# A block of state-space scan, gated mixer and experts: the head of the front stage and the segment sums of the scan are computed in another form and on other engines

## The reference

```python
mod_l = (silu(c) @ ada_w + ada_b);  mod_c = (silu(c_ctx) @ ada_w + ada_b)
xm = rmsnorm(h, norm1_w) * (1 + sc1) + sh1              # for both token sets
xbc, dt_raw = xm @ w_in[:, :2048], xm @ w_in[:, 2048:2080]
xs, bm, cm = split(silu(dwconv_centred(xbc, conv_w, conv_b)))   # 3 taps over the tokens
dt = softplus(dt_raw + dt_bias)                         # 2 directions x 16 heads
# per direction, in chunks of 128 tokens, the context's chunks first:
a_cum = cumsum(dt * A)                                  # A negative
decay[i, j] = exp(a_cum[i] - a_cum[j])  for j <= i, else 0
y_diag = sum_j (cm[i] . bm[j]) * decay[i, j] * dt[j] * x[j]
y_off  = (cm[i] . h_in) * exp(a_cum[i])
h      = h * exp(a_cum[end]) + sum_j bm[j] * exp(a_cum[end] - a_cum[j]) * dt[j] * x[j]
```

## Time and profile before

| | us |
|---|---|
| median of three runs | 3674.97 |
| the profiled execution | 3683.1 |
| its span | 3681.3 |
| TensorE busy | 3352.1 |
| VectorE busy | 1264.4 |
| ScalarE busy | 950.4 |
| GpSimd busy | 276.1 |

### The profile page before, as it was taken

How to read it: one execution, slowest core, us unless ns; L and a number is a source line. 1 busy time by engine, 2 the same in 40 slices (tenths; PEclk the granted TensorE clock), 3 DMA queues, 4 the chain that set the end, 5 groups by cost and what they waited for, 6 DMA issues and landing times.

```text
span 3681.3 us, 36826 instructions
## 1 busy us (share of the span) xinstructions
PE 3352.1 (91%) x14704; PEld 2224.6 (60%) x14704; DVE 1264.4 (34%) x1876; ACT 950.4 (26%) x1555; POOL 276.1 (7%) x241
## 2 busy tenths in 40 slices
PE   5888896999599999799999989999899899989997
PEld 3547643444443443377567858878677477768875
DVE  2237411101301011445433453323454533453334
ACT  2121102000200000244453323221344533232212
POOL 0006302000100000111111000000021111000000
PEclk7997898999799999899999989999899999999998
DMA  5001043220399999321111222223311012322221
GB/s 203 23 9 60 30 169 121 92 88 26 130 385 409 409 409 409 121 69 48 47 52 61 89 70 96 92 82 102 71 58 59 25 62 69 97 69 92 93 86 62
DMA packets 266761, 436.79 MB, mean 119 GB/s; under 512 B 10336, under 2 KB 180704, under 8 KB 265824
## 3 DMA queue, kind: packets, MB, share of 16 engines
q1 hardware_dynamic: 266448, 432.54, 33.3%
q0 software_dynamic: 144, 1.90, 0.1%
HBM read 432.32 MB, written 2.10 MB: 118 GB/s over the span
## 4 chain that ended last, share of the span: by engine, by line
PE 51%; DVE 4%; ACT 2%; DVEq 1%; issue 1%; ACTq 0%; DMA 0%; POOLq 0%; SPq 0%; POOL 0%
PE bank L1879 42%; PE bank L1940 2%; PE bank L1957 1%; PE bank L1976 1%; PE bank L1916 1%; PE bank L1526 1%; DVE ring_r L2211 1%; PE bank L1971 1%; ACT ring_r L2080 1%; PE bank L1946 1%; DVE x L1557 0%; DVE layers_norm_rstd L1554 0%; DVE layers_work L2330 0%; DMA ring<-in_w_in 0%; DVE x_r L1568 0%
## 5 line engine op out<-in xcount | busy, mean ns | idle before, releaser
L1879 PE MATMUL bank<-experts_x_hi_r,ring_r 128*128 128x512 f32 x1720 | 575.5, 400 | 7.0 <-DVE ring_r L2211 7.0
L1879 PE MATMUL bank<-x_r,ring_r 128*128 128x512 f32 x1376 | 545.7, 397 | 0.0
L2211 DVE TENSOR_TENSOR ring_r<-ring,ring_r 128x2048 fp32r<-128x2048 f32 (+2 forms) x162 | 324.4, 2002 | 427.8 <-ACT ring_r L2080 426.6
L1879 PE MATMUL bank<-layers_work_r,ring_r 128*128 128x512 f32 x1312 | 392.3, 401 | 9.2 <-DVE layers_work_r L2354 9.2
L2080 ACT ACTIVATE ring_r<-ring 128x2048 fp32r<-128x2048 f32 (+2 forms) x162 | 272.7, 1684 | 495.3 <-PE bank L1879 475.4
L1879 PEld LDWEIGHTS bank<-experts_x_hi_r,ring_r 128*128 128x128 f32 x1720 | 323.6, 188 | 109.5 <-issue 25.2
L1879 PE MATMUL bank<-ring_r 128*128 128x512 f32 (+1 forms) x1224 | 388.0, 378 | 0.0
L231 PE MATMUL bank<-xm,ring 128*128 128x512 f32 (+1 forms) x832 | 321.3, 546 | 0.0
L1879 PEld LDWEIGHTS bank<-layers_work_r,ring_r 128*128 128x128 f32 x1312 | 249.5, 190 | 78.5 <-DVE layers_work_r L2354 10.1
L1879 PEld LDWEIGHTS bank<-x_r,ring_r 128*128 128x128 f32 x1376 | 258.6, 188 | 62.6 <-issue 1.0
L2403 POOL TENSOR_TENSOR layers_p<-layers_p,layers_recip 128x512 f32<-128x512 f32 (+2 forms) x160 | 145.3, 925 | 1446.8 <-DVEq L2257 1446.8
(11 more groups left out here) (319 smaller groups left out, 4048.3 us busy)
## 6 DMA issues: line engine op xcount, KB each, us to landing
ring<-in_w_in SPq DMA_DIRECT2D x54, 1024.0 KB, 5.3
ring<-in_w_ffn_in SPq DMA_DIRECT2D x44, 1024.0 KB, 5.1
ring<-in_w_gate SPq DMA_DIRECT2D x30, 1024.0 KB, 18.4
ring<-in_w_in SPq DMA_DIRECT2D x14, 2048.0 KB, 8.1
ring<-in_w_down SPq DMA_DIRECT2D x28, 1024.0 KB, 18.5
ring<-in_w_up SPq DMA_DIRECT2D x26, 1024.0 KB, 18.2
ring<-in_ada_w SPq DMA_DIRECT2D x12, 2048.0 KB, 8.7
mixer_kept<-in_w_down SPq DMA_DIRECT2D x24, 1024.0 KB, 18.5
```

Source lines behind the costliest of these rows:

```text
L1879: last = pe.matmul(out, lhs, rhs, start=start and k == 0, stop=stop and k == len(pairs) - 1)
L2211: dve.tensor_tensor(r32(tile), tile, r32(hi), ALU.subtract).then_inc(done, 1)
```

## The change

In `front`: the fourth modulation slab goes to `core.x` and the first slab of w_in to `a.y`, which are idle there, so neither waits for a ring slot; the dt weights come as an array of long rows (1 KB a partition) that is laid out ahead. The sum of squares and the dt product run in four column strips, k-tile by k-tile, with the tokens as the streaming operand; the strips are folded by one product with ones (squares) or turned and added (dt, `turn_dt` and VectorE's `step`). Context squares go to VectorE. x is multiplied by the reciprocal root ahead of the modulation's factors, and what follows them is one tensor_scalar (latent) or one ACTIVATE (context) a k-tile. ScalarE copies the modulation's rows. The softplus runs beside column 1.

In `scan`: the eight curves of 16 heads (4 chunks, 2 directions) are made once by TensorE from a dta spread over 32 partitions a group (`strewn`). Per step ScalarE spreads one curve over four columns of a block diagonal (`stairs`), and `sums_of` is four products of 32 rows and 512 columns with ones. The segments move from VectorE to ScalarE, as Relu(acum - sum) and Exp(-...), and the mask moves into cm . bm, which VectorE multiplies by a triangle once per chunk and direction (`masked`). `sums_of(u+1)` moves between the two halves of `diag(u)`. `xdt` and `xend` get buffers of their own. The two masks leave the constants.

```diff
...
+    ada_w3 = core.x
+    xbc_w0 = a.y[:, :, :].rearrange("p t f -> p (t f)").rearrange("p (k n) -> p k n", k=KD)
...
+    core.slabs.begin(ada[:3] + xbc[1:])
...
+            for s in range(3):
                 load_slab(core, sp, ("ada", s), w_tiles(I["ada_w"], 0, D, 512 * s, 512))
-            load_slab(core, sp, "dtw", w_tiles(I["w_in"], 0, D, XBC, 2 * HEADS))
-            for s in range(4):
+            sp.dma_start(dt_w[:, :, :], I["w_dt"].rearrange("p (k n) -> p k n", k=KD)).then_inc(ada_in, 16)
+            sp.dma_start(ada_w3[:, :, :], w_tiles(I["ada_w"], 0, D, 512 * 3, 512)).then_inc(ada_in, 16)
+            sp.dma_start(xbc_w0, w_tiles(I["w_in"], 0, D, 0, 512)).then_inc(xbc_in, 16)
...
+                rows = slice(32 * (k % 4), 32 * (k % 4) + 32)
+                for name, sq_done, lo, hi in (("sq_l", sq_x, 0, T), ("sq_c", sq_ctx, T, TA)):
+                    pe.wait_ge(sq_done, k + 1)
+                    last = pe.matmul(core.ps(name)[rows, 0:hi - lo], core.c("mean_d")[:, 0:32], squares[:, k, lo:hi],
+                                     start=k < 4, stop=k >= 4)
...
+            pe.wait_ge(strips_kept, 2)
+            for name, lo, hi in (("rms_l", 0, T), ("rms_c", T, TA)):
+                core.banks.vacant(pe, name)
+                pe.matmul(core.ps(name)[:, 0:hi - lo], core.c("ones"), strips[:, 0, lo:hi], start=True, stop=True)\
...
+                else:
+                    pe.wait_ge(ada_in, 32)
...
-            for t in range(TT + CT):
-                last = product(pe, core.ps("dt")[:, t * 32:t * 32 + 32],
-                               [a.xm[:, k, t * P:(t + 1) * P] for k in range(KD)],
-                               [w[:, k, :] for k in range(KD)],
-                               core.slabs.done(("ada", 3)) if t == 0 else None)
...
+            for k in range(KD):
+                rows = slice(32 * (k % 4), 32 * (k % 4) + 32)
+                for name, xm_done, lo, hi in (("dt_l", xm_x, 0, T), ("dt_c", xm_ctx, T, TA)):
+                    pe.wait_ge(xm_done, k + 1)
+                    last = pe.matmul(core.ps(name)[rows, 0:hi - lo], dt_w[:, k, :], a.xm[:, k, lo:hi], start=k < 4, stop=k >= 4)
...
+            for s in range(4):
+                core.banks.filled(act, ("ada", s))
+                if s >= 2:
+                    core.banks.filled(act, ("adt", s - 2))
+                act.activation(ada_rows[:, s % 2, :], core.ps(("ada", s))[:, :], ACT.Identity).then_inc(core.banks.done(("ada", s)), 1)
+                act.drain().then_inc(ada_kept, 1)
...
+                act.activation(a.xm[:, k, T:TA], a.xm[:, k, T:TA], ACT.Identity, scale=scale1[:, k, 1:2],
+                               bias=core.mod[:, k, 1:2]).then_inc(xm_ctx, 1)
...
+            dve.reciprocal(rstd[:, :], rstd[:, :])
+            dve.drain()
+            dve.wait_ge(x_in, 16)
+            for k in range(KD):
+                dve.tensor_tensor(a.xm[:, k, :], a.xm[:, k, :], rstd[:, :], ALU.mult)
...
             for k in range(KD):
-                for j, (lo, hi) in enumerate(((0, T), (T, TA))):
-                    dve.scalar_tensor_tensor(out=a.xm[:, k, lo:hi], in0=a.xm[:, k, lo:hi],
-                                             scalar=scale1[:, k, j:j + 1], in1=rstd[:, lo:hi],
-                                             op0=ALU.mult, op1=ALU.mult).then_inc(scaled, 1)
...
+                dve.tensor_scalar(a.xm[:, k, 0:T], a.xm[:, k, 0:T], scale1[:, k, 0:1], core.mod[:, k, 0:1], ALU.mult, ALU.add)\
...
+                for name, t0, n in (("dt_tl", 0, TT), ("dt_tc", TT, CT)):
+                    core.banks.filled(dve, name)
+                    dve.tensor_reduce(raw[:, t0:t0 + n, :], core.ps(name)[:, 0:n * P].rearrange("p (t j h) -> p t h j", t=n, j=4),
+                                      AX.X, ALU.add).then_inc(core.banks.done(name), 1)
...
+                dve.tensor_tensor(raw, raw, dt_bias.unsqueeze(1).broadcast_to([P, CT + TT, 2 * HEADS]), ALU.add)
...
-    cb = spare[:, 0:TT * GROUPS * P].rearrange("p (t n) -> p t n", t=TT)
-    xdt, xend = spare[:, 2 * D:3 * D], spare[:, 3 * D:4 * D]
+    cb = spare.rearrange("p (d t g j) -> p d t g j", d=2, t=TT, g=GROUPS)
+    xdt, xend = core.sb("xdt", [P, D], ctx), core.sb("xend", [P, D], ctx)
...
+    curve = strewn[:, :, :, :, :].rearrange("p t d g r -> p (t d) (g r)")
+    stair = core.sb("stair", [P, HPG, P], ctx)
...
     core.slabs.begin(MIXER_SLABS)
...
+            for n in (0, 1):
+                core.banks.vacant(pe, ("curve", n))
+                for q in range(4):
+                    td = 4 * n + q
+                    last = pe.matmul(core.ps(("curve", n))[:, q * P:(q + 1) * P], curve[:, td, :],
+                                     core.c("tri_b" if td % 2 else "tri_f"), start=True, stop=True)
+                last.then_inc(core.banks.put(("curve", n)), 1)
...
             def sums_of(u):
-                d, t, _ = steps[u]
+                pe.wait_ge(stair_done, order[u] + 1)
                 for g in G:
                     core.banks.vacant(pe, ("seg", u, g))
-                    for r in range(HPG):
-                        col = d * HEADS + g * HPG + r
-                        last = pe.matmul(core.ps(("seg", u, g))[:, r * P:(r + 1) * P],
-                                         a.dta[:, t, col:col + 1].broadcast_to([P, P]),
-                                         core.c("tri_b" if d else "tri_f"), start=True, stop=True)
-                    last.then_inc(core.banks.put(("seg", u, g)), 1)
+                    rows = slice(32 * g, 32 * g + 32)
+                    pe.matmul(core.ps(("seg", u, g))[:, :], core.c("ones")[rows, :], stair[rows, :, :], start=True, stop=True)\
+                      .then_inc(core.banks.put(("seg", u, g)), 1)
...
-                if u + 1 in outs:
-                    sums_of(u + 1)
...
+                    if half == 0 and u + 1 in outs:
+                        sums_of(u + 1)
...
-            for n in range(len(outs) * GROUPS):
-                act.wait_ge(seg_done, n + 1)
-                act.activation(seg[:, n % NSEG, :], seg[:, n % NSEG, :], ACT.Exp).then_inc(decay_done, 1)
+            for n in (0, 1):
+                core.banks.filled(act, ("curve", n))
+                act.activation(curve[:, 4 * n:4 * n + 4, :], core.ps(("curve", n))[:, :].rearrange("p (q j) -> p q j", q=4), ACT.Identity)\
+                   .then_inc(core.banks.done(("curve", n)), 1)
...
+            def stairs(u):
+                d, t, _ = steps[u]
+                for r in range(HPG):
+                    act.activation(stair[:, r, :], curve[:, 2 * t + d, :], ACT.Identity, scale=core.c("stair")[:, r:r + 1])
+                act.drain().then_inc(stair_done, 1)
...
+                    for r in range(HPG):
+                        col = d * HEADS + g * HPG + r
+                        last = act.activation(seg[:, n % NSEG, r * P:(r + 1) * P], core.ps(("seg", u, g))[:, r * P:(r + 1) * P],
+                                              ACT.Relu, bias=acum[:, t, col:col + 1], scale=-1.0)
+                    last.then_inc(core.banks.done(("seg", u, g)), 1)
+                    act.drain()
+                    act.activation(seg[:, n % NSEG, :], seg[:, n % NSEG, :], ACT.Exp, scale=-1.0).then_inc(decay_done, 1)
+                if u + 1 in outs:
+                    stairs(u + 1)
...
-            def segments(u):
...
-                        last = dve.scalar_tensor_tensor(
-                            out=seg[:, n % NSEG, r * P:(r + 1) * P], in0=core.ps(("seg", u, g))[:, r * P:(r + 1) * P],
-                            scalar=acum[:, t, col:col + 1], in1=core.c("mask_b" if d else "mask_f"),
-                            op0=ALU.subtract, op1=ALU.add)
...
+            def masked(t):
+                core.banks.filled(dve, ("cb", t))
+                for d, tri in enumerate(("tri_f", "tri_b")):
+                    last = dve.tensor_tensor(cb[:, d, t, :, :], core.ps(("cb", t))[:, :].rearrange("p (g j) -> p g j", g=GROUPS),
+                                             core.c(tri).unsqueeze(1).broadcast_to([P, GROUPS, P]), ALU.mult)
+                last.then_inc(core.banks.done(("cb", t)), 1)
...
-            segments(first)
+            for t in range(first, TT):
+                masked(t)
+            dve.drain().then_inc(cb_done, 1)
...
-                if u + 1 in outs:
-                    segments(u + 1)
...
-                    cbg = cb[:, t, g * P:(g + 1) * P].unsqueeze(1).broadcast_to([P, HPG, P])
+                    cbg = cb[:, d, t, g, :].unsqueeze(1).broadcast_to([P, HPG, P])
...
+            pool.memset(strewn[:, :, :, :, :], 0.0).then_inc(strewn_zero, 1)
...
-        "tri_f": lower.T, "tri_b": lower, "mask_f": np.where(lower.T > 0, 0.0, NEG), "mask_b": np.where(lower > 0, 0.0, NEG),
+        "tri_f": lower.T, "tri_b": lower,
+        "stair": (np.arange(P)[:, None] % 32 == np.arange(HPG)[None, :]).astype(np.float32),
...
+    g["w_dt"] = f("w_in")[0][:, XBC:XBC + 2 * HEADS].reshape(KD, P, 2 * HEADS).transpose(1, 0, 2).reshape(P, -1)
```

(50 more changed lines are left out.)

198 lines of the change are left out of this document (93 added, 105 removed).

## The result

The changed kernel takes 3630.9 us (median of 4 runs, 3628.9 to 3633.5) beside 3676.4 for the kernel before (4 runs, 3674.3 to 3679.7): 45.5 us faster, ratio 0.9876, interval 0.9859 to 0.9893. The forecast was 3615, range 3596 to 3643: sign and range held, the gain was a quarter less than the 60 us forecast. Its profiled execution took 3630.0, span 3628.2.

A forecast was written before the change was run, and what follows sets the result against it. The prediction took the front's head to wait on a chain and the scan on hand-overs between engines. Front -33 and scan -27 gave -60 from the median 3675.0, so 3615 us, range 3596 to 3643.

The forecast's parts named there:

- Front: All work ahead of the scan: earlier slab, shorter scaling and turned dt product save 33 us, bounds -36 and -17.
- rival B: Front's dt product: column strips don't overlap, as each feeds two banks; front -17, total -44, 3631 us; chance 0.08.
- The root's slack: Front: reciprocal root and its products end at 38, hidden before the factors at 43.3 with 5 us to spare.
- the slab's 3.5 us: Front: the last modulation slab, no longer waiting for a ring slot, lets TensorE begin at 37.2 instead of 40.75.
- Scan: Scan stage: 126.6 us in place of 153.6, so -27; -44 at a period of 9.6, +4 at 16.4.
- The head: Scan's start: the first step's fourth decay product ends 38.2 us into the stage.
- Period: Scan step: a ring of ScalarE's segments, stair and TensorE's sums, 11.3, plus 0.7 for half clock: 12.0 us, bounds 9.6 and 16.4.
- the tail: Scan's end: half a diagonal 1.0, addition 0.7, L801 2.35 and hand-overs, together 4.4 us.
- a sign of being wrong: Scan: the prediction is wrong if the output steps' additions are 15 us or more apart.
- Rival A: Scan keeps its pace through half-clock spells or a ring through scaled x; scan -3, total -36, 3639 us; chance 0.15.
- Rival C: Scan: GpSimd's bound, a period of 9.6 us, is reached; scan -44, total -77, 3598 us; chance 0.12.
- Rival D: Scan: Relu and Exp in different tables, two loads of 1.28 a group; scan +55, total +22, 3697 us; chance 0.03.

The follow-up runs named there:

- experiment 11: The changed kernel with the fourth modulation slab loaded through the ring again: 3631.2 us, ratio 0.9875 to the kernel before.
- Experiment 4: The changed kernel with two buffers in turn for `part`, the second in a free context tile of x: 3617.4 us, ratio 0.9835 to the kernel before.
- experiment 8: The changed kernel with two `part` buffers, GpSimd's skip products in its waits and each step's fourth decay product on VectorE: 3629.7 us, ratio 0.9869 to the kernel before.
- experiment 5: The changed kernel with two extra TensorE products ahead of the wait for each of the 32 decay products: 3639.5 us, ratio 0.9897 to the kernel before.

## Why the prediction was right in sign and its gain 15 us too large

**Front: -33 forecast, -33.1 in the first trace, -31.5 on average.** Slab at 38.0 (37.2), factors at 42.3 (43.3), tiles ready at 46.4 (47.2), first column product at 47.7 (49.5). The average sets the eleven profiled executions with the new front (scan's first pass at 241.2) against the three with the old one (272.7). The 1.8 us are the clock: in this execution the last slab's 16 passes ran at full (1.92), where the forecast kept half (3.62), and the dt product's last passes did too (1.25 behind the last tile; the forecast's 2.3 lies between its 1.3 and 2.6 without a reason given). In the eleven the slab's passes took 1.92 in four and 2.9 to 3.6 in seven, and the first column product starts at 47.7 to 51.1, mean 49.5. The strips do overlap, over two banks too (32 passes in 4.59, for which one after another would be 10.4): rival B is refuted. The root's slack was 5 us as forecast (VectorE ends its products at 37.3). What the forecast left out is the half clock behind the wait ahead of the third column product, +1.7; from the first column product to the scan the new front takes 1.0 more than the old one, where the forecast's terms say 0.7 less. So the -33.1 of this trace is in part luck: 1.8 too good, 1.7 too bad. And the cause named for the slab's 3.5 us, a place of its own, was not needed (experiment 11). On average the slab came 2.5 earlier (38.5 against 41.1): near the size, not by the mechanism.

**Scan: -27 forecast, -20.2 measured.** The head was right (first step's fourth decay product ends 37.6 into the stage, forecast 38.2). ScalarE's costs came out below the forecast: four segments in 1.13 (1.3), 1.74 a group (2.1), stair 1.26 (1.4). TensorE's sums took 1.13 at full clock, as forecast (1.1), and 2.09 at half. The step that failed is **Period**: "A ring of waits: ScalarE's segments (8.4), its stair (1.4), TensorE's sums to the first bank read", 11.3, and 12.0 us with its 0.7 for half clock. The mean was 12.6 (fourth decay products end at 276.8 and 364.9, seven periods), though ScalarE needs only 4 x 1.74 + 1.3 = 8.3, not 8.4 + 1.4 = 9.8, and was idle for 46 of 101 us: with its pieces as measured that ring would have been 8.3 + 1.5 = 9.8. That 12.0 came so near 12.6 is luck: a ring priced too high stood in for one left out. What set the pace was a ring that the forecast didn't price: GpSimd's addition, VectorE's `part`, and behind it the bank of the fourth sum and scaled x. Experiment 4 removes it and the stage falls to 116.3, below the 126.6 forecast. So 4.1 of the 6.7 us that the stage is too long are the period; 3.3 are the tail, 7.7 in place of 4.4, its diagonal at half clock (6.56), and the head gives 0.6 back. The steps are uneven too: the additions stand 5.4 to 15.9 apart, one over the 15 that the prediction named as a sign of being wrong.

Rival A named lost pace by half-clock spells or by a ring through scaled x; it went over a quarter of that way (7 of 24 us), through another buffer. Rival C, GpSimd's list as the bound, is what experiment 4 points to once the buffer is doubled, at 11.1 and not 9.6, for the decay products cost 1.73 each beside a busy VectorE and 1.24 where it mostly waits (4.95 for four at 333.94 in the changed kernel); experiment 8, which shortened that list, got slower by another path and so didn't confirm it. Rival D: no table load stands among Relu and Exp.

The Trainium skill (TensorE: Matmul & The Clock Gate, on the measured speedup of small-K matmuls) gives 3.07x for four 32-row tiles. The trace agrees: eight passes one after another would be 8 x 0.43 = 3.5 us, and they took 1.13 at full clock, 3.1 times less.

**The total.** Scan 7 short, front 1.5 short by the average: -60 becomes -51.5. The other 6 us of the measured -45.5 are of the size by which the profiled execution of before lay above its median, and by which the untouched rest scatters; which part of it was in the front and which in the rest stays open.

## What to carry to other kernels

When work moves off the engine that was the bound, walk every single buffer and every bank of the loop once round, and price the ring through each, not only the one through the engine that receives the work. A buffer that two less busy engines hand over can hold the busiest one: here 4 KB a partition, found in a dead tile of x, were worth 17 us of the stage, as much as moving the segments to ScalarE. And where TensorE's clock falls behind a gap, as at 333 us here, the wait costs its length and then twice the time of the next products; removing the gap paid (experiment 4), filling it did not (experiment 5).

## What the runs showed of the hardware that was not expected

- Extra passes bring the clock up (0.80 to 0.89 in 290 to 350 us) and the stage was still 10.7 us longer, as they stand ahead of a hand-over.
- 128-column ACTIVATEs with a pointer bias, from a PSUM bank, take 0.36 each and follow each other at 0.25 (four in 1.13).
- The same 3.0 us wait of TensorE in the front left the clock at full in three traces of the old front and was followed by half clock in eleven of the new one.
- Four column strips with 512 columns each: 16 passes in 1.92 at full clock, 3.6 times faster than 16 x 0.43.
- VectorE's and GpSimd's operations with both inputs in SBUF lengthen each other. In the changed kernel scaled x, started together with GpSimd's addition, took 3.42, nearly the sum of both (1.23 + 2.35); where it starts first (experiment 4, at 318.19) it takes 1.23, and GpSimd's next three products 5.69 in place of 3 x 1.27. GpSimd and VectorE of the changed kernel:

```profile
339.51 2.35 POOL L875 TENSOR_TENSOR y<-y,scan_part 128x1024 f32<-128x1024 f32 x1 [0.61 <-DVEq L851]
```
```profile
339.52 3.42 DVE L823 TENSOR_TENSOR scan_xdt<-xtok,dt 128x1024 f32<-128x1024 f32 x1
```
